# Loads of gates and activations, last stores and the return of x moved between queues in the expert down stage

## The reference

```python
def peer(h, p):
    ...
    idx = jnp.take_along_axis(cidx, pos, axis=-1)
    gates = jax.nn.softmax(top_s.astype(F32), axis=-1).astype(h.dtype)
    eu, ev = p['expert_u'], p['expert_v']

    def block(args):
        xb, ib, gb = args
        act = jax.nn.gelu(jnp.einsum('nd,nhkd->nhk', xb, eu[ib]))
        return jnp.einsum('nhk,nhkd->nd', act * gb, ev[ib])
    ...

x = x + gt2 * rmsnorm(peer(h, p), p['g_post2'])
```

## Time and profile before

| | us |
|---|---|
| median of 3 runs | 3016.49 (3008.72 to 3024.49) |
| the profiled execution | 3005.93 |
| its span, first to last instruction | 3004.1 |
| PE busy | 2831.6 (94%) |
| DVE busy | 2173.3 (72%) |
| ScalarE busy | 1224.0 (41%) |
| POOL busy | 860.1 (29%) |
| mean granted PE clock | 0.978 |

### The profile page before, as it was taken

One profiled execution on the slowest core, in us unless ns is written; L12 is line 12 of the kernel. 1 busy time (PEld: TensorE's weight loads), 2 busy tenths in 40 slices (PEclk: granted clock), 3 DMA queues, 4 the chain that ended last, 5 costly groups with the idle time before them and its releaser, 6 DMA issues.

```text
span 3004.1 us, 59572 instructions
## 1 busy us (share of the span) xinstructions
PE 2831.6 (94%) x24170; PEld 2489.1 (83%) x24170; DVE 2173.3 (72%) x3111; ACT 1224.0 (41%) x1857; POOL 860.1 (29%) x552
## 2 busy tenths in 40 slices
PE   7899999899999999889999999999988999999998
PEld 5799999587877879789988888888877878777886
DVE  2455532666666653659978999988878999898998
ACT  3333333333333243433336566654443333333333
POOL 0000000122222220057764444441122344444232
PEclk9999999799999989999999999999999999999999
DMA  9633333243344323336559999999999999999996
GB/s 404 236 128 126 128 126 111 79 146 132 124 152 151 131 115 126 108 140 229 196 208 362 367 395 392 394 400 410 418 405 403 418 417 418 418 417 417 418 418 277
DMA packets 207690, 815.60 MB, mean 271 GB/s; under 512 B 81520, under 2 KB 101104, under 8 KB 118416
## 3 DMA queue, kind: packets, MB, share of 16 engines
q1 hardware_dynamic: 105040, 527.71, 45.4%
q0 software_dynamic: 36864, 268.45, 21.6%
q10 hardware_dynamic: 65600, 16.78, 2.5%
HBM read 772.50 MB, written 40.37 MB: 271 GB/s over the span
## 4 chain that ended last, share of the span: by engine, by line
PE 28%; DMA 14%; DVE 8%; issue 4%; POOL 3%; ACT 1%; SPq 1%; DVEq 0%; ACTq 0%; POOLq 0%
DMA work<-act_table 11%; PE ps L1861 10%; PE ps L1862 5%; POOL wlo L1843 3%; PE ps L2246 2%; PE ps L2247 2%; PE ps L2248 2%; DVE x L2395 2%; DVE wlo L1843 1%; DVE work L2504 1%; PE ps L2141 1%; PE ps L2142 1%; PE ps L2143 1%; DMA act_table<-act_f 1%; DVE wlo L2509 1%
## 5 line engine op out<-in xcount | busy, mean ns | idle before, releaser
L1861 PE MATMUL ps<-hboth,whi 128*128 128x512 f32 x1664 | 589.6, 397 | 13.3 <-DVE wlo L1843 13.3
L1862 PE MATMUL ps<-hboth,wlo 128*128 128x256 f32 x1664 | 466.0, 280 | 0.0
L2246 PE MATMUL ps<-whi,hboth 128*128 128x512 f32 x1024 | 403.8, 394 | 32.8 <-DVE wlo L2509 19.9
L2285 POOL DMA_INDIRECT work<-expert_v,idx x128 | 285.5, 2231 | 448.4 <-DVE work L2504 423.0
L2247 PE MATMUL ps<-wlo,hboth 128*128 128x512 f32 x1024 | 401.3, 392 | 0.0
L2248 PE MATMUL ps<-whi,hboth 128*128 128x512 f32 x1024 | 400.8, 391 | 0.0
L1861 PEld LDWEIGHTS ps<-hboth,whi 128*128 128x128 f32 x1664 | 312.7, 188 | 84.7 <-DVE wlo L1843 15.6
L2285 POOL DMA_INDIRECT x<-u_rows,idx x128 | 236.4, 1847 | 433.5 <-DVE x L2395 251.2
L1862 PEld LDWEIGHTS ps<-hboth,wlo 128*128 128x128 f32 x1664 | 314.9, 189 | 0.0
L2504 DVE SCALAR_TENSOR_TENSOR work<-work,dots 128x2048 f32<-128x2048 f32 x127 | 297.8, 2345 | 0.1
L1843 POOL TENSOR_TENSOR wlo<-raw,whi 128x2048 fp32r<-128x2048 f32 x38 | 189.2, 4983 | 262.3 <-ACT whi L1848 262.3
(11 more groups left out here) (373 smaller groups left out, 6169.2 us busy)
## 6 DMA issues: line engine op xcount, KB each, us to landing
raw<-expert_u SPq DMA_DIRECT2D x94, 1024.0 KB, 8.1
x<-w_ada SPq DMA_DIRECT2D x64, 1024.0 KB, 5.2
work<-expert_v SPq DMA_DIRECT2D x64, 1024.0 KB, 14.7
raw<-expert_v SPq DMA_DIRECT2D x64, 1024.0 KB, 14.7
raw<-w_in SPq DMA_DIRECT2D x50, 1024.0 KB, 4.8
raw_more<-expert_u SPq DMA_DIRECT2D x34, 1024.0 KB, 8.7
z<-w_ada SPq DMA_DIRECT2D x32, 1024.0 KB, 13.7
raw<-w_out SPq DMA_DIRECT2D x16, 1024.0 KB, 4.7
```

Of the source, the lines that this page charges most:

```text
L1861: pe.matmul(both, whi[:, r, k, :], hboth[:, :, k, CTX:T], start=(k == 0), stop=False)
L1862: last = pe.matmul(both[:, 0], wlo[:, r, k, :], hhi[:, k, CTX:T], start=False, stop=(k == KD - 1))
L2246: pe.matmul(bank, ah, vh[:, part], start=first, stop=False)
L2285: nc.gpsimd.indirect_dma_start(out=buf, out_offset=None, in_=rows, in_offset=bass.IndirectOffsetOnAxis(ap=idx[:, s:s + 1], axis=0)).then_i ...
```

## The change

SP no longer stores the last five slices of activations; ScalarE does so from its own queue, each behind the GELU that made it. SP's load of x from `x_kept` comes behind its whole loop over the blocks instead of ahead of it. And the loads of gates and activations of groups 2 to 63 are issued by ScalarE (`next_group`): in its period g, behind the conversion of the first block, those of group g+2, after a wait for `act_split` of group g. Ahead of the first of them ScalarE waits until both tables are whole in DRAM (`tables_whole`). The loads of groups 0 and 1 stay with SP. The number of buffers, the DVE, PE and POOL programs and the bytes moved don't change.

```diff
--- before.py
+++ after.py
@@ -1919,38 +1919,26 @@
                 with sp.Fori(0, TURNS) as it:
                     rest(it)
                 load_fixed(M_DOWN - 1)
-                spill(NK - 5)
                 for r in range(2):
                     sp.wait_ge(stage_out[r].sem, 16 * (SETS // 2))
                     sp.wait_ge(spilled[r].sem, 16 * 2)
                 groups(0, 0)
                 load_v(expert_v[0], 0)
                 load_v(expert_v[1], 1)
-                spill(NK - 4)
                 groups(1, 2)
-                spill(NK - 3)
                 for r in range(2):
                     sp.wait_ge(w_low[r].sem, M_DOWN // 2)
                     load_v(expert_v[2 + r], 2 + r)
-                    spill(NK - 2 + r)
-                for r in range(2):
-                    sp.wait_ge(spilled[r].sem, 16 * (NK // 2))
-
+                def down(it):
+                    for n in range(4):
+                        sp.wait_ge(w_low[n % 2].sem, it * 2 + (M_DOWN // 2 + 1 + n // 2))
+                        load_v(expert_v[bass.ds(it * 4 + (4 + n), 1)].rearrange("o i d -> (o i) d"), n)
+
+                with sp.Fori(0, NK // 4 - 1) as it:
+                    down(it)
                 sp.wait_ge(ug_used.sem, SLOTS)
                 sp.wait_ge(x_saved.sem, 16)
                 sp.dma_start(x[:, :, :], x_kept).then_inc(x_back.sem, 16)
-
-                def down(it):
-                    for n in range(4):
-                        if n % 2 == 0:
-                            j = n // 2
-                            sp.wait_ge(act_split.sem, it * 2 + (j + 1))
-                            groups(j, it * 4 + (2 * j + 4))
-                        sp.wait_ge(w_low[n % 2].sem, it * 2 + (M_DOWN // 2 + 1 + n // 2))
-                        load_v(expert_v[bass.ds(it * 4 + (4 + n), 1)].rearrange("o i d -> (o i) d"), n)
-
-                with sp.Fori(0, NK // 4 - 1) as it:
-                    down(it)
                 for k in range(0, KD, 4):
                     sp.wait_ge(added_back.sem, 4 + 2 * (k // 4 + 1))
                     sp.dma_start(y_out[:, k:k + 4, :], x[:, k:k + 4, :]).then_inc(stores_y.sem, 16)
@@ -2062,8 +2050,14 @@
                 with act.Fori(0, TURNS) as it:
                     for n in range(TURN_OF):
                         rest(it, n)
+                def spill_own(g):
+                    act.wait_ge(u_out.sem, g + 1)
+                    act.dma_start(act_table[:, g, :], act_f[:, g % 2]).then_inc(spilled[g % 2].sem, 16)
+
+                spill_own(NK - 5)
                 for n in range(REST - TURNS * TURN_OF):
                     rest(TURNS, n)
+                    spill_own(NK - 4 + n)
                     if n == 2:
                         act.wait_ge(gated_.sem, 1)
                         nc.scalar.activation(act_hi[:, 0], by_tile(act_in[:, 0]), ACT.Copy).then_inc(act_high.sem, 1)
@@ -2071,7 +2065,19 @@
                 nc.scalar.activation(dots[:, :], dots[:, :], ACT.Gelu_apprx_tanh).then_inc(weights_in.sem, 1)
                 nc.scalar.activation(tok_part[:, 0, 0:1], eps[:, 0:1], ACT.Sqrt)
 
-                def period(it, j, more=True):
+                def next_group(it, j):
+                    act.wait_ge(act_split.sem, it * 2 + (j + 1))
+                    for dst, table in ((gate_in, gate_table), (act_in, act_table)):
+                        act.dma_start(dst[:, j].rearrange("p e t -> p (e t)"),
+                                      table[:, bass.ds(it * 4 + (2 * j + 4), 2), :].rearrange("p e t -> p (e t)")
+                                      ).then_inc(gate_landed[j].sem, 16)
+
+                def tables_whole():
+                    for r in range(2):
+                        act.wait_ge(stage_out[r].sem, 16 * (SETS // 2))
+                        act.wait_ge(spilled[r].sem, 16 * (NK // 2))
+
+                def period(it, j, more=True, fetch=True, first=False):
 
                     if more:
                         act.wait_ge(gated_.sem, it * 2 + (j + 2))
@@ -2083,13 +2089,17 @@
                             act.wait_ge(v_landed[r].sem, it * 16 + (16 * j + 16 if j else 16))
                             act.wait_ge(prod.sem, it * 4 + (M_DOWN + 2 * j + e + 1))
                             nc.scalar.activation(whi[:, e], v_raw[r], ACT.Copy).then_inc(w_high.sem, 1)
-
-                period(0, 0)
+                            if e == 0 and fetch:
+                                if first:
+                                    tables_whole()
+                                next_group(it, j)
+
+                period(0, 0, first=True)
                 period(0, 1)
                 with act.Fori(1, GROUPS // 2 - 1) as it:
                     period(it, 0)
                     period(it, 1)
-                period(GROUPS // 2 - 1, 0)
+                period(GROUPS // 2 - 1, 0, fetch=False)
 
                 def sum_squares(tile):
                     for c in range(4):
```

More of the change, by code:

```diff
@@ L1934, in _ @@
                     load_v(expert_v[2 + r], 2 + r)
-                    spill(NK - 2 + r)
-                for r in range(2):
-                    sp.wait_ge(spilled[r].sem, 16 * (NK // 2))
-                sp.wait_ge(ug_used.sem, SLOTS)
-                sp.wait_ge(x_saved.sem, 16)
-                sp.dma_start(x[:, :, :], x_kept).then_inc(x_back.sem, 16)
                 def down(it):
                     for n in range(4):
-                        if n % 2 == 0:
-                            j = n // 2
-                            sp.wait_ge(act_split.sem, it * 2 + (j + 1))
-                            groups(j, it * 4 + (2 * j + 4))
                         sp.wait_ge(w_low[n % 2].sem, it * 2 + (M_DOWN // 2 + 1 + n // 2))
@@ L1953, in _ @@
                     down(it)
+                sp.wait_ge(ug_used.sem, SLOTS)
+                sp.wait_ge(x_saved.sem, 16)
+                sp.dma_start(x[:, :, :], x_kept).then_inc(x_back.sem, 16)
                 for k in range(0, KD, 4):
```

## The result

| | before | after |
|---|---|---|
| median of 6 runs each, us | 3012.29 (3006.23 to 3024.49) | 3192.31 (3177.35 to 3210.19) |
| ratio, 95% interval | | 1.0583 [1.0556, 1.0609] |
| profiled execution's span, us | 3004.1 | 3192.9 |
| granted TensorE clock over the span | 0.978 | 0.958 |

The account below looks back on a forecast made before the run. Three resources within ten per cent, DMA on top at 418 GB/s, bounded the kernel. 3005.93 + 167 (longer periods) - 8 (start) + 1 (x's return) = 3166; the median lies 10.6 higher, 3176 us, range 3045 to 3275.

Parts of the forecast that it names:

- rival (a): Down stage: L 7.3 to 9.5, clock falling in some/most periods, T 13.0 to 15.1, 3115 to 3243 us; chance 0.64.
- T: One period of the down stage, a group of two products; 11.27 us before, 14.0 forecast.
- L: Down stage, time from issue of a load of activations to its landing, on ScalarE's queue; 8.3 us taken.
- The ring: Down stage: second-row `v_low`, two products, conversion, load issue, landing, `gate`, `weigh`, `v_low`; two periods long, binds above L 3.8.
- signs named: Down stage: DVE idle before `gate` 3+ us, loads every 14 us, some 340 GB/s, PE's `v_low` waits, clock below 1.
- (18.7 + L)/2: Down-stage period: 18.7 us of other legs plus landing L, over two periods; T = 13.5 at L = 8.3.
- PE's clock: Down stage, PE standing once a period: a slow product adds 3.1 us; 0.5 taken, T 14.0 instead of 13.5.
- first leg: Down stage, `v_low` to load issue: products 0.05 + 10.88, conversion 0.05 + 1.92, issue 0.6; 13.5 us.
- the 1.3 us for start and receipt: Part of L in the down stage, taken from the first such load, which found SP's queue empty; 1.3 us.
- 12 packets of one rival and 4 of two: Packet part of L in the down stage: 12 packets against one rival queue, 4 against two; 4.3 + 2.7 us.
- Part 2: Last stores on ScalarE, start of down stage: first `gate` at about 2267.5 instead of 2275.52; -8 us, bounds 0 and -18.4.
- Part 3: x's return behind the blocks, end of down stage: hidden, takes turns with the last gathers; +1 us (0 to 5).

Follow-up runs that it names:

- earlier: Changed kernel with each load of gates and activations issued one period earlier, still on ScalarE's queue: 3006.44 us, ratio 0.9988.
- loads_only: Changed kernel with last stores and x's return put back, only the loads of gates and activations on ScalarE: 3188.69 us, ratio 1.0582.
- no_gathers: Changed kernel with only the first 4 of the 128 gathers of `expert_v`: 3027.31 us, ratio 1.0033.
- one_load: Changed kernel without the loads of gates of groups 2 to 63, only those of activations issued: 3113.4 us, ratio 1.032.
- pe_busy: Changed kernel with 6 useless matmuls per iteration on PE between the two products: 3189.7 us, ratio 1.0612.
- sp_late: Changed kernel with the loads of gates and activations back on SP's queue, issued late behind the first low part: 3350.32 us, ratio 1.1105.
- stores_x: Kernel before with x's return behind the loop and the last five stores of activations on ScalarE, loads still on SP: 3005.22 us, ratio 0.9961.
- x_later: Changed kernel with x's return held back until the last `gate` is done: 3188.86 us, ratio 1.0528.
- stores_first: Kernel before with x's return behind the loop and two of SP's last stores of activations moved ahead on SP: 3005.64 us, ratio 0.9977.
- x_only: Kernel before with only x's return moved behind SP's loop over the blocks: 3003.42 us, ratio 0.9976.

## Why the prediction was right, and where it was wrong

The time is in the range and rival (a) came true in T, between 13.0 and 15.1, measured 14.06, and in the clock, which fell in most turns; its L of 7.3 to 9.5 was missed narrowly, with 9.8. Point by point:

**The ring and its cause: right.** Five of the signs named are there: DVE's idle time before `gate` (206 us in total over all, before 50), the issue of loads every 14 us, 334 GB/s at a share of 0.85, PE's waits for `v_low`, and a clock of 0.92. *earlier* shows that the moment makes it and not the queue, *loads_only* that it is part 1. The stalls are distributed differently than forecast, 2 to 12 us in every second period instead of some 3 in each, which changes no sum since the ring is two periods long. There are two rings, one through the even and one through the odd groups, and from group 9 on that of the odd groups binds every time. Of its 27 loads 25 are issued right behind a block and wait 3.0 us and more for their first packet, while those of all even groups start after 1.0 to 1.3 us.

**The terms of (18.7 + L)/2: two errors that cancelled, and the clock on top.** Means over the 27 turns of groups 9, 11 and so on to 61, in all of which `gate` waits, against the forecast:

| term of two periods, us | forecast | measured |
|---|---|---|
| `v_low` to issue of the load, clock at 1.00 | 13.5 | 11.85 |
| L of the loads that bind | 8.3 | 9.8 (5.7 to 15.3) |
| landing to the next `v_low` | 5.2 | 5.2 |
| PE's clock | 1.0 | 1.4 |
| sum | 28.0 | 28.3 |

That the sum came out so close is luck: the first two lines are off by 1.65 and 1.5 us in opposite directions. The first leg was too long by 1.65 us. The step that failed is "ScalarE converts, 0.05 + 1.92" ahead of the issue: the load goes out while the conversion runs. In the rows above, the conversion starts at 2645.44 and the issues at 2645.59 and 2646.01. The code puts the issue behind the conversion, but in 46 of the change's 62 pairs of loads it starts before the conversion has ended. L was too short by 1.5 us, and the part of it that was mis-sized is the 1.3 us for start and receipt. It came from the first load of the stage, whose queue was empty; the loads that bind take 2.9 us to their first packet and 0.8 behind the last, 3.7 together. The part for the packets was a little too long instead, 7.0 against 6.1. The forecast let a load meet 12 packets of one rival and 4 of two, thus 20 of the others on each engine, and it met 13.8. That queues take turns by count rests on the earlier trace rows alone, 385 and 381 packets in the same 8 us. *no_gathers* (L 5.7 instead of 9.8) shows what goes with the gathers, and *one_load* that the packets are not the whole of L. The single landings go from 5.7 to 15.3 us, and no run here shows the length of a turn.

**The clock: right in kind, too small.** The 3.1 us of a slow product in the forecast rest on the earlier trace rows, where the clock was 1.00 behind a gap of 1.79 us and 0.51 in 2782 to 2784, behind one of 2.69 us. The timeline of PE in the kernel before has the starts behind that second gap, 0.43 us apart at first and 0.23 a little later:

```profile
2782.19 0.63 PE L2247 MATMUL ps<-wlo,hboth 128*128 128x512 f32 x1
2782.62 0.63 PE L2248 MATMUL ps<-whi,hboth 128*128 128x512 f32 x1
...
2785.09 0.39 PE L2247 MATMUL ps<-wlo,hboth 128*128 128x512 f32 x1
2785.32 0.39 PE L2248 MATMUL ps<-whi,hboth 128*128 128x512 f32 x1
```

Some 15 matmuls at 0.2 us more each are the 3.1 us. The gap of 2.6 us that the forecast had at T = 13.5 is nearer to the second of the two; that a third of the periods lose it was an estimate. In the change the leg with the clock at 1.00 is 11.85 us, the mean over the 27 turns 13.26, so the fall goes with 1.4 us in two periods, against the 1.0 taken. The alternation goes with it: one gap in two periods instead of 2.6 us in each. In 19 of the turns it is 2.6 to 10.2 us long and the clock falls, in the 8 others it is 0 to 2.7 us and the clock stays at 1.00. The windows above show one: behind a gap of 10.17 us the clock is 0.50 at 2607 to 2611 and back at 1.00 at 2613. This is read from the trace; *pe_busy*, which was to confirm it, put its own matmuls in the place of the slow ones, so the clock's share as time of the kernel stays open.

**The loop's sum.** The forecast counted 61 periods, 61 x 2.73 = 167 us. The first 60 of them gave 60 x (14.06 - 11.26) = 168 against 164; the 61st is that from group 62 to 63, which gave 15.8 against 2.7 (under part 3).

**Part 2: wrong in size, -8 forecast.** I had the first of the stores wait at most 1 us for DVE. It stood 7.22 us in ScalarE's queue, and ScalarE was idle for 7.35 us of the up stage's last slices. SP's first load of activations, which waits for the 4 MB store, goes out 9.8 us later than before (2241.67 against 2231.91). Of these, 5.5 us was already the lag of the up stage in these two executions (ScalarE's `gelu` of slice 123 starts at 2228.20 against 2222.68), in front of anything the change touches. The other 4.2 us can't be put on part 2. From that `gelu` to SP's first load of gates it is 13.1 us in the change and 12.9 to 13.2 in *sp_late* and *stores_x*, but 8.5 to 9.1 in *earlier*, *no_gathers*, *pe_busy* and *x_later*, which have the same stores on ScalarE; before it was 8.9, and in *stores_first*, without them, 18.2. The block whose transfer I had named as next late did decide, it took 21.8 us (2244.05 to 2265.85) as the one in the earlier trace rows took 22.0. Then the load of group 2, for which I had set 8.3 - 2, took 12.74 us: it met both rivals (6.7 packets of the gathers and 17.9 of SP's queue on each engine, beside its own 16), near the 12.1 us that had been worked out for that case. Without the 5.5 us the first `gate` is 0.9 us early instead of 8 (2.2 in *x_later*, which has the same program up to there). The other traces, counted from the same `gelu`, say where the -8 went: the first `gate` is 6.4 us early in *x_only* and 5.5 in *stores_x*, so the gain at the head is that of x's leaving and the stores add none to it, and it is 3.0 us late in *loads_only*, a cost of part 1 at the head that the forecast had left out.

**Part 3: wrong, +1 forecast.** x's return is hidden from the sum over x, for which nobody waited, but I looked for its victim in the gathers. It was the last load of activations, issued 1 us behind it and in the ring: 19.4 us of landing. *x_later* puts 8.5 us on it, outside my bound of 5. The rest of the 15.8, 7.3 us, is what a turn's stall costs in this last period, in which in the kernel before there was none.

**The sum of span** is 168 - 0.9 + 15.8 + 0.3 = 183 us from that `gelu` on, and 5.5 that were there before it; the forecast had 160. By the medians the difference is 180. Of the 23 us between 183 and 160 the first 60 periods are 4; the others are the two ends of the stage.

## What to carry to other kernels

When a load is moved, write down which event lets it out and which event needs it, and follow the ring until it closes: the sum of its legs over the number of periods that it spans is the new period, whatever the engines' busy times say. A turn of one period (*sp_late*, 16.7 us) hurts twice as much as one of two with the same landing. Lead is worth more than a quick queue: loads that took 16 us with a lead of as much cost nothing that the kernel before didn't also pay, loads that took 10 with a lead of some 2 cost 5.8%. And when a load's landing is estimated from a load that found its queue empty, look in the trace for what is issued just ahead of it: here that added over 2 us to the load in the ring.

## What the runs showed of the hardware

- In the change 46 of the 62 pairs of loads on ScalarE's queue were issued before the conversion ahead of them had ended. In the turn shown the issue came 0.15 us after the start of a conversion of 1.93 us (2645.44, 2645.59).
- The 4 MB store of gates passed on ScalarE's queue as 16384 packets of 256 bytes, the last of them at 2240.8 in the change. The first store of activations behind it, issued at 2228.65, stood 7.22 us, and ScalarE sat idle for 7.35 us; in *stores_x* it stood 7.49 us, in *earlier* 6.60 and in *pe_busy* 3.94. In *one_load*, where the 4 MB store had landed 21.6 us before, it took 0.40 us. The second store of the change took 0.34 us (2238.48) while packets of the 4 MB store still passed, so what let the first one go isn't shown.
- L of a load of activations (256 KB), by company: 5.7 us in the median of *no_gathers*, beside the blocks alone; 9.8 in the mean of the binding loads of the change, beside blocks and gathers with DMA at 0.85; 15.2 in the median of the kernel before, on SP's queue with DMA at 1.02; 19.4 for the one beside x's return of 3 MB. In *earlier*, on ScalarE's queue with DMA at 1.01, the load at 2601.65 took 16.2 us from its issue to the `gate` that waited for it.
- A load on ScalarE's queue started later where SP had just issued a block of 1 MB: first data packet 3.0 to 4.0 us after the issue (25 pairs, block at most 1.3 us before), against 1.0 to 1.3 us (28 pairs) in the same stage of the change.
- Behind a gap of 2.56 us PE's clock stayed at 1.00 (the turn from 2634.22 is 11.8 us long to the issue), behind another gap of 2.56 us in the same stage, before 2549.46, it fell (0.50 in 2551 to 2553, and 13.4 us). In the earlier trace rows 2.69 us was enough. The length of the gap alone doesn't decide here.
